# Issuing a request for expert weights only when the last but one of those already issued has landed

## The chip, the cores and the metric

The kernel runs on one core of a Trainium2 chip. The metric is the device time of one execution in microseconds (us), lower is better. Instructions are written by hand for each engine (TensorE = PE, VectorE = DVE, ScalarE = ACT, GpSimd = POOL, SyncE = SP), and the engines wait for each other on semaphores that the code names and counts itself. Transfers from DRAM are requested by SP, almost all of them, in program order, on one hardware queue that 16 DMA engines serve.

## The reference, cut to what matters

Two layers over 256 tokens of 1024 features, in float32. Each layer is a mixing part (gating, attention and retention between two projections) and then a mixture of 16 experts. What bears on the change is the expert part:

```python
for e in range(N_EXPERTS):                      # 16
    he = jax.nn.silu(t @ w_gate[e]) * (t @ w_up[e])
    y = y + combine[:, e:e + 1] * (he @ w_down[e])
```

`w_gate[e]` and `w_up[e]` are 1024 x 512 and `w_down[e]` is 512 x 1024, so each of the three is 2 MB. A token uses two experts, but over 256 tokens all 16 are used, so each layer reads 16 x 3 x 2 MB = 96 MB of expert weights. After the second layer a last RMSNorm is applied.

## The kernel before, in words

The expert part works through **items**. An item is a pair of experts with up to 64 tokens (slots) for each; there are 8 items a layer with these inputs, 16 in all. For an item PE makes the gate product, the up product (both line 1106), turns the hidden tile, and makes the down product (line 1135). It needs three weight tiles of 4 MB: gate, up and down, each requested in two parts of 2 MB. For most items (`load_experts`, lines 417 to 423) the parts are the two experts. For items 1, 2 and 3 and for every fourth item (`load_halves`, lines 403 to 415) they are the two halves of the rows of both experts, and for up and down of every fourth item the second half is requested as two quarters of 1 MB (line 412), the last of which has a semaphore of its own.

There are two buffers for gate (`gate_b`, `gate_a`, by turns) and one each for up and down. So SP requests the gate of an item when PE is done with the gate of two items before (semaphore `gated`), and up and down when PE is done with the part of the item before (`upped`, `downed`). These waits on used buffers are the only ones that the requests have:

```python
for e in experts:
    sp.dma_start(dst[:, e], src[...]).then_inc(loaded[e].sem, 16)
```

SP runs through one program in order: for layer 0 the mixing weights (`load_piece`, lines 385 to 401), then gate, up and down of item 0 and gate of item 1 (lines 442 to 453), a wait for the number of items (line 455), then lines 471 to 478 for gate of items 2 and 3 and up and down of items 1 to 3, then the loop of line 479 for four items a turn (lines 480 to 486; it runs once a layer here). Then it goes on to the mixing weights of layer 1, which reuse the up and down buffers, and at the end to the four stores of the output (line 492). A request that waits holds back all that follow.

Each request adds 16 to its `loaded` semaphore, one for each DMA engine that has landed its share, and PE waits for the full count before the first product that reads the part (lines 1101, 1103, 1139, 1150 and 1153). A wait of SP is followed by `settle`, an increment of a semaphore that nobody reads.

Of the kernel before, what the change touches and what calls it, by code (L numbers as in the profile page):

```python
# [118 lines left out]
def hybrid_trunk(nc, x_in, norm1, w_in, a_ln_g, a_ln_b, a_ws, a_bs, ret_gn, w_out, norm2, router_g, router_gb,  # L119
                 router_e, router_eb, w_gate, w_up, w_down, final_norm, table, out):  # L120
    ctx = ExitStack()
    with ctx:
# [8 lines left out]
        def settle(eng):  # L131

            eng.sem_inc(settled.sem)
# [10 lines left out]
        gate_w = [gate_b.rearrange("p (e c n) -> p e c n", e=2, c=DC), gate_a]  # L144
# [3 lines left out]
        up_w = sb("up_w", [P, 2, DC, HID])  # L148
        up_at = nc.sbuf_base - 4 * 2 * DC * HID
        down_w = sb("down_w", [P, 2, HC, D])  # L150
# [149 lines left out]
        gate_loaded = [[signal(f"gate_loaded{o}{b}", 16) for b in range(2)] for o in range(2)]  # L300
        up_loaded = [signal(f"up_loaded{b}", 16) for b in range(2)]
        down_loaded = [signal(f"down_loaded{b}", 16) for b in range(2)]
        up_last, down_last = signal("up_last", 16), signal("down_last", 16)

        gated, upped, gate_tanh = signal("gated", 2, 8), signal("upped", 2, 8), signal("gate_tanh", 1)
        gate_open = signal("gate_open", 1)
        he_ready, he_turned, heT_ready = signal("he_ready", 1), signal("he_turned", 1), signal("heT_ready", 1)
        downed, y_summed = signal("downed", 2, 8), signal("y_summed", 1)
# [12 lines left out]
        gate_d = w_gate.rearrange("l (q e) (p c) n -> (l q) p e c n", e=2, c=DC)  # L321
# [55 lines left out]
        @block.sync  # L377
        def _(sp):
            sp.dma_start(x[:], x_in.rearrange("b (t p) d -> p (b t) d", p=P)).then_inc(x_loaded.sem, 16)
            sp.wait_ge(range_zeroed.sem, 1)  # L380
            for l in range(DEPTH):

                first = 0 if l == 0 else sp.value_load(items[0:1, 1:2], min_val=0, max_val=4 * PAIRS * DEPTH)

                def load_piece(j, src):
                    if j < 2:

                        sp.wait_ge(upped.sem, upped.at(first, 0))
                    elif j < 4:

                        sp.wait_ge(downed.sem, downed.at(first, 0))
                    else:

                        sp.wait_ge(projected.sem, projected.at(l, j - 3))
                    settle(sp)
                    if j == BQ:
                        for b in range(2):
                            half = slice(None), slice(4 * b, 4 * b + 4), slice(None)
                            sp.dma_start(piece[j][half], src[half]).then_inc(bq_loaded[b].sem, 16)
                        return  # L400
                    sp.dma_start(piece[j], src).then_inc(piece_loaded[j].sem, 16)

                def load_halves(dst, src, loaded, used, g, q, back=0, quarter=None):

                    quarters = dst.shape[2] // 4
                    for b in range(2):
                        sp.wait_ge(used.sem, used.at(g, b + 1 - back * used.turn))
                        settle(sp)
                        if b == 1 and quarter is not None:
                            for k, signalled in ((2, loaded[1]), (3, quarter)):  # L410
                                rows = slice(k * quarters, (k + 1) * quarters)
                                sp.dma_start(dst[:, :, rows], src[bass.ds(q, 1), :, :, rows].rearrange("q p e c n -> (q p) e c n")).then_inc(signalled.sem, 16)
                            continue
                        rows = slice(2 * b * quarters, 2 * (b + 1) * quarters)
                        sp.dma_start(dst[:, :, rows], src[bass.ds(q, 1), :, :, rows].rearrange("q p e c n -> (q p) e c n")).then_inc(loaded[b].sem, 16)

                def load_experts(dst, src, loaded, used, g, q, back=0, experts=(0, 1)):

                    if used is not None:
                        sp.wait_ge(used.sem, used.at(g, 2 - back * used.turn))  # L420
                        settle(sp)
                    for e in experts:
                        sp.dma_start(dst[:, e], src[bass.ds(q, 1), :, e].rearrange("q p c n -> (q p) c n")).then_inc(loaded[e].sem, 16)

                for j in range(6):
                    load_piece(j, w_in_p[bass.ds(l, 1), :, :, PIECE_COL[j]:PIECE_COL[j] + COLS]
                               .rearrange("l p c n -> (l p) c n"))
                    if l == 0 and j == BK:
                        sp.dma_start(const[:, CONST_FIRST:], table[:, CONST_FIRST:]).then_inc(const_loaded.sem, 16)
                for n in range(2):  # L430
                    if n == 1:

                        sp.wait_ge(gelu_done.sem, gelu_done.at(l, 1))
                        sp.wait_ge(proj_copied_a.sem, proj_copied_a.at(l, CQK))
                        for k in range(4):
                            there, here = slice((k ^ 1) * HD // 2, ((k ^ 1) + 1) * HD // 2), slice(k * HD // 2, (k + 1) * HD // 2)
                            sp.dma_start(work1[there], qkc[here].rearrange("p c t -> p (c t)")).then_inc(swapped.sem, 16)
                    load_piece(6 + n, w_out_p[bass.ds(l, 1), :, :, n * COLS:(n + 1) * COLS]
                               .rearrange("l p c n -> (l p) c n"))

                sp.wait_ge(projected.sem, projected.at(l, BV + 1))
                load_experts(up_w, up_d, up_loaded, upped, first, l * PAIRS, 1)
                sp.wait_ge(attended.sem, attended.at(l, 2))
                settle(sp)
                load_experts(gate_w[0], gate_d, gate_loaded[0], None, None, l * PAIRS)

                load_experts(gate_w[1], gate_d, gate_loaded[1], None, None, l * PAIRS + 1, experts=(0,))
                for n in range(2):
                    sp.wait_ge(out_done.sem, out_done.at(l, T + n + 1))
                    settle(sp)  # L450
                    load_experts(down_w, down_d, down_loaded, None, None, l * PAIRS, experts=(n,))
                    if n == 0:
                        load_experts(gate_w[1], gate_d, gate_loaded[1], None, None, l * PAIRS + 1, experts=(1,))

                sp.wait_ge(items_ready.sem, items_ready.at(l, 1))
                settle(sp)
                last = sp.value_load(items[0:1, 1:2], min_val=PAIRS, max_val=4 * PAIRS * DEPTH)

                def pair(g):
                    return sp.snap((g & (PAIRS - 1)) + l * PAIRS)  # L460

                def load_gate(g, o, load=load_halves):
                    load(gate_w[o], gate_d, gate_loaded[o], gated, g, pair(g), 2)

                def load_up(g, load=load_halves, **quarter):
                    load(up_w, up_d, up_loaded, upped, g, pair(g), 1, **quarter)

                def load_down(g, load=load_halves, **quarter):
                    load(down_w, down_d, down_loaded, downed, g, pair(g), 1, **quarter)

                load_gate(first + 2, 0)
                load_up(first + 1)
                load_down(first + 1)
                load_gate(first + 3, 1)
                load_up(first + 2)
                load_down(first + 2)
                load_up(first + 3, quarter=up_last)
                load_down(first + 3, quarter=down_last)
                with sp.Fori(first + 4, last, 4) as g0:
                    for i in range(3):  # L480
                        load_gate(g0 + i, i % 2, load_experts)
                        load_up(g0 + i, load_experts)
                        load_down(g0 + i, load_experts)
                    load_gate(g0 + 3, 1)
                    load_up(g0 + 3, quarter=up_last)
                    load_down(g0 + 3, quarter=down_last)

            out_t = out.rearrange("b (t p) d -> p (b t) d", p=P)
            for n in range(2):
                for t in range(T):  # L490
                    sp.wait_ge(out_ready[t].sem, n + 1)
                    sp.dma_start(out_t[:, t, n * COLS:(n + 1) * COLS], h[:, t, n * COLS:(n + 1) * COLS]).then_inc(out_stored[t].sem, 16)
            for t in range(T):
                sp.wait_ge(out_stored[t].sem, 32)
# [1119 lines left out]
```

## Time and profile before

| what | us |
|---|---|
| median of 3 runs | 693.33 (692.57 to 695.35) |
| the profiled execution, its own time | 693.77 |
| its span | 692.0 |
| PE busy (share of the span) | 658.4 (95%) |
| DMA packets of SP's queue, share of 16 engines' span | 85.5% |

A busy share is a mean over the span; the expert part of layer 0 lies at about 130 to 340 us and that of layer 1 at about 470 to 680 us. A row of the stretches view gives a stretch in us from the span's start, the busy time of each engine in it with the number of instructions, the granted clock of TensorE (1.00 is full), the share of time in which the 16 DMA engines were busy, and the rate in GB/s. A row of the issues view names the tile, the issuing queue, the kind, the count, the size of each and the time from issue to landing.

### The profile page before, as it was taken

Reading aid. Unit: us, or ns where it says so; the run is one execution under the profiler, and the core shown is the slowest. Engines: PE = TensorE matmul, PEld = TensorE weight load, DVE = VectorE, ACT = ScalarE, POOL = GpSimd, SP = SyncE. Lnnn points to the kernel's source line nnn. Section 1 sums busy time; section 2 is a strip of 40 time slices with the busy share of each in tenths; the row PEclk is TensorE's granted clock in tenths of the full one; section 3 lists DMA queues with packets and bytes.
Section 4 is the critical chain, followed back from the end, with each engine's and each line's share of the span. In section 5 each row is a group of like instructions: output and inputs, shape, how many; then the busy total and the mean of one; then the engine's idle time right before and its main releaser. Section 6 shows DMA issues by size and latency. Waiting matters only on the chain.

```text
span 692.0 us, 9069 instructions
## 1 busy us (share of the span) xinstructions
PE 658.4 (95%) x3466; PEld 383.4 (55%) x3466; DVE 303.0 (44%) x634; ACT 195.9 (28%) x344; POOL 17.4 (3%) x29
## 2 busy tenths in 40 slices
PE   6999999999999997999999999999999999989993
PEld 5888878653443542543488878784543453353431
DVE  3769985611232221321475898673221331231234
ACT  4557543421111210211164564342211111111102
POOL 2110000200000000000001000000000000000000
PEclk9999999999999999999999999999999999999997
DMA  9983259999999999999987341997999999999992
GB/s 332 322 313 107 109 209 429 379 415 403 423 416 423 426 426 430 426 423 419 398 311 240 130 152 32 410 430 322 422 420 421 416 428 427 429 427 425 422 411 83
DMA packets 40906, 241.94 MB, mean 350 GB/s; under 512 B 2688, under 2 KB 2880, under 8 KB 24864
## 3 DMA queue, kind: packets, MB, share of 16 engines
q1 hardware_dynamic: 39680, 239.19, 85.5%
q0 software_dynamic: 1040, 2.04, 1.2%
q8 instruction: 28, 0.46, 0.3%
q10 hardware_dynamic: 144, 0.13, 0.1%
q14 instruction: 14, 0.11, 0.0%
HBM read 239.26 MB, written 1.05 MB: 347 GB/s over the span
## 4 chain that ended last, share of the span: by engine, by line
PE 65%; DMA 22%; DVE 8%; ACT 2%; issue 2%; SPq 0%; DVEq 0%; ACTq 0%
PE psum L1106 24%; DMA up_w<-in_w_up 17%; PE psum L779 16%; PE psum L1135 9%; DMA down_w<-in_w_down 3%; PE psum L1044 3%; PE psum L1083 2%; DVE piece_lo L1220 2%; DMA up_w<-in_w_in 2%; PE psum L1008 1%; PE psum L804 1%; PE psum L759 1%; PE psum L949 1%; DMA x<-in_x 1%; PE psum L868 1%
## 5 line engine op out<-in xcount | busy, mean ns | idle before, releaser
L1106 PE MATMUL psum<-up_w,xT 128*64 128x512 f32 x512 | 114.8, 601 | 8.2 <-DMA up_w<-in_w_up 8.2
L1135 PE MATMUL psum<-down_w,scores 128*64 128x512 f32 x512 | 113.3, 594 | 0.8 <-DMA down_w<-in_w_down 0.8
L779 PE MATMUL psum<-piece_hi,hT_part 128*128 128x512 f32 x320 | 100.3, 394 | 0.0
L1106 PEld LDWEIGHTS psum<-up_w,xT 128*64 128x64 f32 x512 | 39.5, 138 | 80.4 <-issue 76.7
L1135 PEld LDWEIGHTS psum<-down_w,scores 128*64 128x64 f32 x512 | 37.5, 137 | 63.8 <-issue 62.5
L1557 DVE TENSOR_TENSOR y_lo<-psum,y_hi 128x512 fp32r<-128x512 f32 x32 | 22.1, 691 | 102.6 <-ACT y_hi L715 102.6
L779 PEld LDWEIGHTS psum<-piece_hi,hT_part 128*128 128x128 f32 x320 | 58.9, 188 | 12.8 <-issue 1.3
L779 PE MATMUL psum<-piece_lo,hT_part 128*128 128x512 f32 x160 | 62.4, 390 | 0.0
L1106 PE MATMUL psum<-gate_a,xT 128*64 128x512 f32 x256 | 56.4, 593 | 1.1 <-DMA gate_a<-in_w_gate 1.1
L1106 PE MATMUL psum<-gate_b,xT 128*64 128x512 f32 x256 | 56.4, 593 | 0.0
L1536 DVE SCALAR_TENSOR_TENSOR work<-work,psum 128x512 f32<-128x512 f32 x16 | 11.0, 687 | 100.8 <-ACT work L704 100.8
L1539 DVE SCALAR_TENSOR_TENSOR work<-work,slot_scales,psum 128x512 f32<-128x512 f32 x16 | 12.0, 748 | 97.7 <-PE psum L1106 97.7
L715 ACT ACTIVATE y_hi<-psum 128x512 fp32r<-128x512 f32 x32 | 19.1, 597 | 97.1 <-PE psum L1135 97.1
L708 ACT ACTIVATE scores<-psum 128x512 f32<-128x512 f32 x16 | 9.6, 597 | 121.1 <-PE psum L1120 121.1
L1531 DVE TENSOR_TENSOR x<-psum,x 128x512 f32<-128x512 f32 x64 | 40.9, 683 | 3.2 <-PE psum L1083 3.2
L1220 DVE TENSOR_TENSOR piece_lo<-down_w,piece_hi 128x2048 fp32r<-128x2048 f32 x16 | 36.2, 2285 | 10.0 <-ACT piece_hi L560 10.0
L1106 PEld LDWEIGHTS psum<-gate_a,xT 128*64 128x64 f32 x256 | 19.7, 137 | 36.7 <-issue 36.7
L1106 PEld LDWEIGHTS psum<-gate_b,xT 128*64 128x64 f32 x256 | 18.9, 137 | 34.8 <-issue 33.0
L704 ACT ACTIVATE work<-psum,slot_scales 128x512 f32<-128x512 f32 x16 | 11.0, 687 | 89.5 <-PE psum L1106 89.3
L779 PEld LDWEIGHTS psum<-piece_lo,hT_part 128*128 128x128 f32 x160 | 30.0, 188 | 6.5
L560 ACT ACTIVATE piece_hi<-down_w 128x2048 fp32r<-128x2048 f32 x16 | 29.9, 1909 | 4.9 <-DMA down_w<-in_w_in 4.9
L1220 DVE TENSOR_TENSOR piece_lo<-up_w,piece_hi 128x2048 fp32r<-128x2048 f32 x12 | 27.1, 2286 | 2.8 <-ACT piece_hi L560 2.7
(250 smaller groups left out, 860.9 us busy)
## 6 DMA issues: line engine op xcount, KB each, us to landing
up_w<-in_w_up SPq DMA_DIRECT2D x28, 2048.0 KB, 15.4
down_w<-in_w_down SPq DMA_DIRECT2D x28, 2048.0 KB, 14.1
gate_b<-in_w_gate SPq DMA_DIRECT2D x16, 2048.0 KB, 15.9
gate_a<-in_w_gate SPq DMA_DIRECT2D x16, 2048.0 KB, 19.0
up_w<-in_w_in SPq DMA_DIRECT2D x6, 2048.0 KB, 12.7
down_w<-in_w_in SPq DMA_DIRECT2D x4, 2048.0 KB, 20.2
down_w<-in_w_out SPq DMA_DIRECT2D x4, 2048.0 KB, 7.8
up_w<-in_w_up SPq DMA_DIRECT2D x8, 1024.0 KB, 16.0
```

The source lines that it names most:

```text
L560: act.activation(piece_hi[HI_BUFFER[j]][:, 4 * b:4 * b + 4, :], piece[j][:, 4 * b:4 * b + 4, :], ACT.Copy).then_inc(piece_hi_ready.sem, 1)
L704: act.activation(sig, psum[:, 0, :], ACT.Tanh, scale=slot_scales[:, i % 2, 0:1]).then_inc(gate_tanh.sem, 1)
L715: act.activation(y_hi[:, n * COLS:(n + 1) * COLS], psum[:, 2 + n, :], ACT.Copy).then_inc(y_hi_ready.sem, 1)
L779: ins = pe.matmul(o, tokens, w[b][:, c, :], start=(c == 0 and n == 0), stop=(c == DC - 1 and n == len(parts) - 1))
L1044: ins = pe.matmul(gather_out(q, b, c), part[:, t, c, :], pick[:, t, experts].rearrange("p e s -> p (e s)"), start=(t == 0 and part is x_hi ...
L1083: ins = pe.matmul(psum[:, added_bank(i, n, t), :], pickT[:, i % 2, t, :], part[:, n * COLS:(n + 1) * COLS], start=(part is y_hi), stop=(pa ...
L1106: ins = pe.matmul(psum[e * SLOTS:(e + 1) * SLOTS, bank, :], xT[:, c, k:k + SLOTS], w[:, e, c, :], start=(c == 0), stop=(c == DC - 1))
L1135: ins = pe.matmul(psum[e * SLOTS:(e + 1) * SLOTS, 2 + n, :], heT[:, c, e * SLOTS:(e + 1) * SLOTS], down_w[:, e, c, n * COLS:(n + 1) * COLS ...
L1220: V.tensor_tensor(piece_lo[j][part], piece[j][part], piece_hi[HI_BUFFER[j]][part].bitcast(F32), ALU.subtract).then_inc(piece_split.sem, 1)
L1531: V.tensor_tensor(xs, psum[:, added_bank(i, n, t), :], xs, ALU.add).then_inc(x_added.sem, 1)
L1539: V.scalar_tensor_tensor(he, sig, slot_scales[:, i % 2, 1:2], psum[:, 1, :], ALU.mult, ALU.mult).then_inc(he_ready.sem, 1)
L1557: V.tensor_tensor(y_lo[:, ys], psum[:, 2 + n, :], y_hi[:, ys].bitcast(F32), ALU.subtract).then_inc(y_lo_ready.sem, 1)
```

## The change

From `load_up` of item 2 on, every part waits, after its buffer is free, for the landing of an earlier part: part k waits for part k of the tile requested just before. As a tile has two parts, that is the last but one of the parts issued. Gate waits for down of the item before, up for gate, down for up. Where a second half is issued as two quarters, the wait stands before the first of them, and the landing of its fourth quarter is not among the landings waited for.

```diff
+                def landed(before, k):
+
+                    if before is not None:
+                        signals, g, each, ahead = before
+                        sp.wait_ge(signals[k].sem, g * each + (ahead + 16))
+                        settle(sp)
+
-                def load_halves(dst, src, loaded, used, g, q, back=0, quarter=None):
+                def load_halves(dst, src, loaded, used, g, q, back=0, before=None, quarter=None):
...
                         sp.wait_ge(used.sem, used.at(g, b + 1 - back * used.turn))
                         settle(sp)
+                        landed(before, b)
...
-                def load_experts(dst, src, loaded, used, g, q, back=0, experts=(0, 1)):
+                def load_experts(dst, src, loaded, used, g, q, back=0, before=None, experts=(0, 1)):
...
                     for e in experts:
+                        landed(before, e)
                         sp.dma_start(dst[:, e], src[bass.ds(q, 1), :, e].rearrange("q p c n -> (q p) c n")).then_inc(loaded[e].sem, 16)
...
-                load_up(first + 2)
-                load_down(first + 2)
-                load_up(first + 3, quarter=up_last)
-                load_down(first + 3, quarter=down_last)
+                load_up(first + 2, before=(gate_loaded[1], first, 8, 16))
+                load_down(first + 2, before=(up_loaded, first, 16, 32))
+                load_up(first + 3, before=(down_loaded, first, 16, 32), quarter=up_last)
+                load_down(first + 3, before=(up_loaded, first, 16, 48), quarter=down_last)
                 with sp.Fori(first + 4, last, 4) as g0:
-                    for i in range(3):
-                        load_gate(g0 + i, i % 2, load_experts)
-                        load_up(g0 + i, load_experts)
-                        load_down(g0 + i, load_experts)
-                    load_gate(g0 + 3, 1)
-                    load_up(g0 + 3, quarter=up_last)
-                    load_down(g0 + 3, quarter=down_last)
+                    for i in range(4):
+                        load = load_experts if i < 3 else load_halves
+                        load_gate(g0 + i, i % 2, load, before=(down_loaded, g0, 16, 16 * (i - 1)))
+                        load_up(g0 + i, load, before=(gate_loaded[i % 2], g0, 8, i // 2 * 16), **({} if i < 3 else dict(quarter=up_last)))
+                        load_down(g0 + i, load, before=(up_loaded, g0, 16, 16 * i), **({} if i < 3 else dict(quarter=down_last)))
```

`load_gate`, `load_up` and `load_down` pass `before` on. No other engine's program is changed, nor the order, number, size or place of any transfer.

## Rows read from the trace of the kernel before

**Rows 1.** The page: 40 slices of the span, DMA queues, and two lines of DMA issues.

```profile
DMA  9983259999999999999987341997999999999992
GB/s 332 322 313 107 109 209 429 379 415 403 423 416 423 426 426 430 426 423 419 398 311 240 130 152 32 410 430 322 422 420 421 416 428 427 429 427 425 422 411 83
...
q1 hardware_dynamic: 39680, 239.19, 85.5%
...
up_w<-in_w_up SPq DMA_DIRECT2D x28, 2048.0 KB, 15.4
...
gate_a<-in_w_gate SPq DMA_DIRECT2D x16, 2048.0 KB, 19.0
```

**Rows 2.** Stretches: full queue, and the places where it ran thin.

```profile
core 0: us, PE busy (x) PEld busy (x) DVE busy (x) ACT busy (x) POOL busy (x), PEclk, DMA share, GB/s
139.00:156.00 17.00, 17.00 (x112) 8.90 (x110) 3.37 (x6) 4.01 (x10) 0.00 (x0) 1.00 1.01 424
158.00:160.00 2.00, 2.00 (x12) 0.75 (x10) 0.69 (x1) 0.63 (x2) 0.00 (x0) 1.00 0.79 307
270.00:310.00 40.00, 39.05 (x194) 18.40 (x195) 9.49 (x16) 5.42 (x11) 0.00 (x0) 0.96 1.01 426
474.00:476.00 2.00, 2.00 (x12) 0.65 (x10) 0.48 (x3) 0.00 (x0) 0.00 (x0) 1.00 0.00 0
476.00:677.00 201.00, 195.72 (x1004) 84.05 (x1000) 47.39 (x80) 27.82 (x58) 0.00 (x0) 1.00 1.00 418
674.00:677.00 3.00, 3.00 (x18) 1.09 (x14) 0.01 (x1) 0.00 (x0) 0.00 (x0) 1.00 0.55 220
```

**Rows 3.** Waits of PE for transfers, 475 to 692 us.

```profile
PE psum L1106 <- DMA up_w<-in_w_up: 4.7, 4, 2.7
PE psum L1135 <- DMA down_w<-in_w_down: 0.4, 1, 0.4
PE psum L1106 <- DMA gate_a<-in_w_gate: 0.2, 1, 0.2
```

**Rows 4.** SP's issues in order of time: start, us, what (first of each pair).

```profile
148.08 0.37 SPq L415 DMA_DIRECT2D up_w<-in_w_up  x1
156.59 3.80 SPq L415 DMA_DIRECT2D down_w<-in_w_down  x2
222.43 0.81 SPq L423 DMA_DIRECT2D up_w<-in_w_up  x2
236.46 0.33 SPq L423 DMA_DIRECT2D down_w<-in_w_down  x1
262.19 0.33 SPq L423 DMA_DIRECT2D gate_b<-in_w_gate  x1
307.63 0.37 SPq L412 DMA_DIRECT2D up_w<-in_w_up  x1
332.12 0.38 SPq L399 DMA_DIRECT2D up_w<-in_w_in  x1
475.17 3.72 SPq L415 DMA_DIRECT2D gate_b<-in_w_gate  x2
478.50 0.39 SPq L415 DMA_DIRECT2D gate_b<-in_w_gate  x1
```

**Rows 5.** Issues view: issues of 148.08, 156.59, 222.85, 236.46, 262.19, 307.63, 475.17, 478.50 us.

```profile
up_w<-in_w_up SPq DMA_DIRECT2D x1, 2048.0 KB, 12.5
...
down_w<-in_w_down SPq DMA_DIRECT2D x1, 2048.0 KB, 9.6
...
up_w<-in_w_up SPq DMA_DIRECT2D x1, 2048.0 KB, 17.9
...
down_w<-in_w_down SPq DMA_DIRECT2D x1, 2048.0 KB, 9.2
...
gate_b<-in_w_gate SPq DMA_DIRECT2D x1, 2048.0 KB, 28.2
...
up_w<-in_w_up SPq DMA_DIRECT2D x1, 1024.0 KB, 19.8
...
gate_b<-in_w_gate SPq DMA_DIRECT2D x1, 2048.0 KB, 7.3
...
gate_b<-in_w_gate SPq DMA_DIRECT2D x1, 2048.0 KB, 8.9
```

**Rows 6.** The chain that ended last, 651 us to the end: start, us, what.

```profile
651.18 0.05 issue
651.23 0.03 SPq L415
651.25 0.04 issue
651.29 20.61 DMA down_w<-in_w_down
671.90 0.24 issue
672.14 7.19 PE psum L1135 x32
...
687.36 0.66 DVEq L122
```

More of the change, by code:

```diff
@@ L460, in pair, with load_gate, load_up, load_down @@
                     return sp.snap((g & (PAIRS - 1)) + l * PAIRS)
[L462 to L469, printed above, removed]
+                def load_gate(g, o, load=load_halves, before=None):
+                    load(gate_w[o], gate_d, gate_loaded[o], gated, g, pair(g), 2, before)
+                def load_up(g, load=load_halves, before=None, **quarter):
+                    load(up_w, up_d, up_loaded, upped, g, pair(g), 1, before, **quarter)
+                def load_down(g, load=load_halves, before=None, **quarter):
+                    load(down_w, down_d, down_loaded, downed, g, pair(g), 1, before, **quarter)
                 load_gate(first + 2, 0)
```

## The prediction

> **What bounds the kernel now.** I read the 40 slices first. In the expert part of each layer the DMA row stands at 9 throughout, at some 420 GB/s, and 239 MB of the traffic is on SP's one queue [rows 1]. PE is nearly as busy, so the next question is which of the two sets the end. From 476 to 677 us the 16 DMA engines are busy 1.00 of the time, while PE is busy 195.7 of 201 us [rows 2] and its idle time there is spent on transfers, 5.3 us [rows 3]. PE begins the layer with weights already in place, catches up with the stream and then waits for it. The chain agrees: its last transfer, a part of down issued at 651.29, takes 20.6 us, and PE's last down product runs on it [rows 6]. So the end of a layer is the start of its stream of requests plus bytes over rate. From 475.17 on, 40 parts of 2 MB (84 MB) follow; at 418 GB/s that is 201 us [rows 2]. Only a DMA engine that idles, or runs at another rate, can move the end.
>
> **Is the order or the depth of the queue what makes a part late?** The second part of gate issued at 262.19 takes 28.2 us to land [rows 4, 5]. Is that slow sharing, or a line? Two parts issued into a short queue give the unit: 475.17 + 7.3 = 482.5 and 478.50 + 8.9 = 487.4, so 4.9 us per part [rows 4, 5]. With the queue empty (share 0.00 from 474 to 476, [rows 2]) one part takes 7.3 us: 4.9 of transfer and 2.4 fixed. 28.2 less 2.4 is 25.8, or 5.3 parts: it stands behind somewhat over four others and then takes its own 4.9. So requests are served one after the other; a deep queue is waiting time, not a slower transfer. Shortening it makes issue to landing short (about 2 x 4.9 = 10 us) by issuing later, and leaves the landing where it is.
>
> **The change, part by part.**
>
> *Rate with two in flight.* Nothing is removed or reordered; parts are issued later. From 139 to 156 us the trace has this very state by accident: each part is issued with one or two others pending, and the rate is 424 GB/s at share 1.01. With three to five pending, 270 to 310 us, it is 426 at 1.01 [rows 2]. Cost of two instead of five: nothing within 0.5%; the cover is the other part in flight.
>
> *Is the cover long enough?* After the change a part is issued when the last but one lands, so one part, 4.9 us, is left. Off this goes the reaction: 0.24 us from a landing to the waiting engine's start, and 0.11 us from a release to SP's issue [rows 6], together 0.35 as an upper bound for the new wait with its settle. 4.55 us remain, and the fixed time to bridge is 2.4: margin 2.1 us for each of the 64 new waits (per layer 4 tiles x 2 in the part before the loop and 12 tiles x 2 in it). The other rows: the part issued at 236.46 had only the one issued at 222.85 ahead of it, landing 17.9 later at 240.75, a cover of 4.3 us, and it landed at 245.7, one unit later: no loss [rows 4, 5]. But the part issued at 156.59 had a cover of 4.0 us (148.08 + 12.5 = 160.6) and landed at 166.2, 5.6 us after, 0.7 us more than the unit [rows 4, 5]; the engines were busy only 0.79 of 158 to 160 us [rows 2]. So the price of one new wait is bounded by 0 (236.46) and 0.7 us (156.59). I take 0: the new cover of 4.55 us is nearer to 4.3 than to 4.0, and 478.50, with a cover of 4.0 us like the bad case, lost nothing. In all, eight parts of the trace were issued with a single one ahead and a cover of 3.9 to 4.7 us; three of them stand in the rows, seven of the eight lost nothing.
>
> *The Trainium skill, weighed.* The fixed 2.4 us is from an idle memory. "DMA: Bandwidth & Descriptors", section "Latency and other measured facts", says that an access to HBM takes 0.2 us on average and 2 us at high load, which the queue of this kernel has all the time. By that page an estimate of the fixed part is 2.4 + 1.8 = 4.2 us, and the margin is 0.35 instead of 2.1; the sum stays 0, but hardly. The late start at 156.59 would fit it, the one at 236.46 does not show it.
>
> *Fast DMA engines.* A landing counts when the slowest of 16 has landed. At the end of the stream, 674 to 677 us, the share falls to 0.55 while the last part is still coming [rows 2]: some engines are 2 us or more ahead. After the change these wait for the slowest one at each part. That costs nothing as long as the slowest is never idle, and it gives nothing either: the rate falls with the share (220/0.55 = 400 against 418/1.00, and 307/0.79 = 389), so an engine does not get faster when others idle. What is lost is some of their lead, which takes up a delay of one engine; I take 0.3 us a layer, between 0 and the 0.7 of the one such event priced above.
>
> *SP itself.* 64 waits, 64 settles and some register arithmetic, with 24 register waits per layer in the loop. SP waits anyway for buffers; between two issues of a pair it needs 0.4 us [rows 4] against 4.9 a part. Cost 0. Behind SP's new waits stand, in its own queue: the next parts (above), the mixing weights of layer 1 and the output. The last new wait of layer 0 is for the third quarter of up, issued at 307.63 and landed at 327.4; the mixing weights are issued at 332.12 when PE is done with the buffer [rows 4, 5]: 4.7 us to spare. The output is stored after the last product. POOL's and ACT's queues are not passed.
>
> *Who waits for a later issue?* PE alone, and it waits for landings, which stay.
>
> Sum: 0 + 2 x 0.3 = 0.6 us at most on 693.77 of the profiled execution, which is 0.4 above the median of 693.33. Put on the median: 693.9, and as the 0.6 is an upper value I say 693.6.
>
> **The rivals.**
>
> *Slower: the queue runs dry between parts.* Each new wait moves an issue back, that of 262.19 by some 18 us (290.4 less two units), so each part now depends on one cover. Where the fixed time exceeds 4.55 us, all 16 engines stop. For: the event at 156.59. Against: seven short covers of the trace without loss. It decides from a fixed time of 4.6 us. If one wait in eight lost 0.7 us, as one short cover in eight of the trace does, the sum is 64/8 x 0.7 = 5.6 us, so 699.3; if all did, 45 us, which I hold for excluded by the stretch from 139 to 156 us. Chance 0.15.
>
> *Faster: fewer requests in flight make the stream smoother.* Engines kept within a part of each other would all finish together, and the spread of 2 us that is exposed at each layer's end (share 0.55 for 3 us is 1.35 us of full rate) would go. For: the spread is there. Against: idle engines do not speed up the others [rows 2]. If it did come: 2 x 1.35 = 2.7 us, up to 4 with a better rate: 690.5. Chance 0.12, of which I put 0.08 beyond 0.5%, as its price lies on that bound.
>
> *The wait hardly ever binds.* Where buffers come free later than the landing, the change does nothing. At 236.46 the landing wait would have been met already. But most parts are issued with three or more pending (28.2 us is one), so it binds for most. It gives 693.4, inside my forecast.
>
> **How the numbers follow.** Forecast of no change: 0.73, with a range of its own of 692 to 696 (the runs shown spread over 692.6 to 695.4, plus the 0 to 1.4 us of lost lead). Slower rival 0.15, faster rival 0.12. To hold 8 in 10 the range reaches toward the rivals: 690.5 to 698. A measurement of this kernel can tell about 0.5%, 3.5 us, from no change. Slower by more: 0.15. Faster by more: 0.08. Within: 0.77.
>
> **What the changed profile would show.** Issue to landing of the expert parts at about 10 us instead of 15 to 19 [rows 1], with the landings themselves in place; SP's own waits moving from PE to DMA; the stream of layer 1 at share 1.00 and 418 GB/s; PE's wait for transfers still near 5 us. A DMA share under 0.98 in the expert part, or units over 4.9 us, would prove me wrong downward; PE waiting less, or units under 4.9, upward.

## The result: 4.4 us slower

| | us |
|---|---|
| before, median of 7 runs | 693.15 (691.82 to 695.35) |
| changed, median of 7 runs | 697.53 (697.27 to 699.71) |
| ratio, 95% interval | 1.0071 (1.0062 to 1.0080) |
| profiled execution of the changed kernel | 697.49, span 695.7 |

The time lies in the range of the prediction (690.5 to 698) and on the side of its first rival: the prediction put 0.77 on a change within 0.5%, and the kernel is 0.7% slower.

The page of the changed kernel, its DMA slices, queues, last chain and issues, against [rows 1]:

```profile
DMA  9993269999999999999997441997999999999992
GB/s 336 326 325 108 82 240 432 359 425 418 411 369 408 425 423 418 424 415 410 401 342 214 155 152 32 389 431 323 423 421 420 411 425 428 419 430 424 421 412 84
...
q1 hardware_dynamic: 39680, 239.19, 85.4%
...
PE 47%; DMA 40%; DVE 8%; ACT 2%; issue 2%; SPq 0%; DVEq 0%; ACTq 0%
...
up_w<-in_w_up SPq DMA_DIRECT2D x28, 2048.0 KB, 9.9
...
gate_a<-in_w_gate SPq DMA_DIRECT2D x16, 2048.0 KB, 11.2
```

From issue to landing a part takes 9.9 us instead of 15.4, and the packets are the same, so the change does what it says. DMA stands at 9 as before. But the rate of slices 11 and 12 (about 174 to 209 us) is 411 and 369 GB/s where it was 423 and 416. The stretches view of the changed kernel:

```profile
139.00:156.00 17.00, 17.00 (x110) 8.89 (x108) 3.36 (x6) 4.01 (x10) 0.00 (x0) 1.00 1.01 426
160.00:180.00 20.00, 20.00 (x102) 8.01 (x100) 4.51 (x7) 1.73 (x4) 0.00 (x0) 1.00 1.01 421
185.00:211.00 26.00, 24.51 (x120) 10.25 (x118) 6.82 (x13) 2.93 (x6) 0.00 (x0) 1.00 0.99 378
270.00:310.00 40.00, 37.19 (x194) 16.93 (x191) 8.19 (x14) 5.51 (x11) 0.00 (x0) 1.00 1.00 419
480.00:680.00 200.00, 195.67 (x994) 84.08 (x992) 47.41 (x80) 27.83 (x58) 0.00 (x0) 0.99 1.00 419
678.00:681.00 3.00, 3.00 (x16) 1.17 (x14) 0.00 (x0) 0.00 (x0) 0.00 (x0) 1.00 0.42 169
```

and of the kernel before, for the stretch that was not shown:

```profile
185.00:211.00 26.00, 25.58 (x128) 10.22 (x126) 7.09 (x14) 2.92 (x6) 0.00 (x0) 1.00 1.01 419
```

Up to 180 us, where the first new wait binds (the up of item 2, issued at 175.10 instead of 170.32), the two streams agree. From 185 to 211 us the changed one has 378 GB/s against 419, with the share of busy time almost the same, 0.99 against 1.01. From 270 to 310 it is 419 against 426 [rows 2]. In this profiled execution layer 0 ends its stream 3.0 us later (last landing 343.1 against 340.1 us). From first landing to last, layer 0 takes 242.6 us against 238.8 and layer 1 238.4 against 238.2, so nearly the whole loss of this execution is in layer 0. The chain that ended last now goes through SP, where the new waits are seen:

```profile
646.08 9.54 DMA gate_a<-in_w_gate
655.66 0.05 issue
655.71 0.03 SPq L423
655.74 0.04 issue
655.77 9.79 DMA up_w<-in_w_up
665.60 0.04 issue
665.64 0.03 SPq L423
665.67 0.04 issue
665.71 9.92 DMA down_w<-in_w_down
```

From a landing to the next issue 0.15 us pass (655.62 to 655.77), less than the 0.35 of the prediction. SP is not what costs the time.

**Where a landing is late.** I took the landing of each part less that of the part before it. The median step is 4.9 us (parts by expert), 4.97 (halves) or 2.55 (quarters); a step longer by over 0.12 us is a late landing. From 180 us in layer 0 and from 510 us in layer 1 the kernel before has 3 of them, 1.3 us together; the changed kernel has 13, 6.6 us together. Of these 6.6 us, 6.2 are at parts in whose last 1.5 to 9.5 us an instruction fetch of 8 or 16 KB began. Such windows cover 42% of the stretches, so a coincidence would give 2.8; moved by a common time, the fetches reach 6.2 us in under 1% of the shifts. The other traces agree: with two in flight in the loop only, or with the idle code of experiment 4, 10 and 12 late landings, 5.4 and 5.2 us together; with three and four in flight 4 and 2, 2.1 and 0.5 us together. One pair, the changed kernel first (issues of 166.19 and 175.10, DMA queues of 179 to 181.5 us), then the kernel before (issues of 166.89 and 170.32, same stretch):

```profile
gate_a<-in_w_gate SPq DMA_DIRECT2D x1, 2048.0 KB, 13.8
...
up_w<-in_w_up SPq DMA_DIRECT2D x1, 2048.0 KB, 11.4
...
q8 instruction: 1, 0.02, 2.7%
```

```profile
gate_a<-in_w_gate SPq DMA_DIRECT2D x1, 2048.0 KB, 14.2
...
up_w<-in_w_up SPq DMA_DIRECT2D x1, 2048.0 KB, 15.8
...
q8 instruction: 1, 0.02, 2.7%
```

Changed: 180.0, then 186.5, a step of 6.5 us. Before: 181.1, then 186.1, a step of 5.0. The same fetch of 16 KB is in both (a packet of 1.1 us on one DMA engine); only the changed kernel pays for it. A fetch hits one engine of 16. If that engine is ahead of the slowest, the landing does not move.

Each part has 16 landings, one for each engine, and they show it: one engine fell back by 1.5 us in both kernels, before one that was 2.0 us ahead of the slowest, in the changed kernel the slowest itself. From 160 us up to there no engine of the changed kernel had lacked work, and most had a lead of 1.3 to 2.1 us. So this hit is not the work of the new wait; as far as the trace shows it is chance. What follows it is: the others are now 1.7 to 3.6 us ahead and have only one part to work on, the next being issued at 186.56. From 187 to 189 us, changed, then before:

```profile
187.00:189.00 2.00, 2.00 (x12) 0.65 (x10) 0.00 (x0) 0.00 (x0) 0.00 (x0) 1.00 0.89 328
```

```profile
187.00:189.00 2.00, 2.00 (x12) 0.72 (x10) 0.00 (x0) 0.00 (x0) 0.00 (x0) 1.00 1.02 426
```

Down to 10 of the 16 engines are at work there. Counted over the stretch from 180 us to 5 us before the last landing of layer 0, the kernel before never has fewer than 16 packets in work, nor has three in flight; the changed kernel has fewer for 11.2 us of 158, mostly 14 or 15, and never none.

### The profile page after: what moved, and what is told of

Same layout as the page of the kernel before. It is cut to its first block, busy times and chain, and to the rows that moved or that the text cites. A ratio compares the mean times of both kernels' runs of the same rounds, so it can differ in the third digit from the quotient of the medians.

```text
span 695.7 us, 9150 instructions
## 1 busy us (share of the span) xinstructions
PE 660.0 (95%) x3466; PEld 385.9 (55%) x3466; DVE 303.0 (44%) x634; ACT 196.1 (28%) x344; POOL 17.0 (2%) x29
## 4 chain that ended last, share of the span: by engine, by line
PE 47%; DMA 40%; DVE 8%; ACT 2%; issue 2%; SPq 0%; DVEq 0%; ACTq 0%
PE psum L786 16%; DMA up_w<-in_w_up 13%; DMA down_w<-in_w_down 13%; PE psum L1113 11%; DMA gate_a<-in_w_gate 7%; PE psum L1142 6%; DMA gate_b<-in_w_gate 4%; DVE piece_lo L1227 2%; DMA up_w<-in_w_in 2%; PE psum L1051 2%; PE psum L1015 1%; PE psum L766 1%; PE psum L811 1%; PE psum L956 1%; PE psum L1090 1%
## 5 line engine op out<-in xcount | busy, mean ns | idle before, releaser
L1113 PE MATMUL psum<-gate_a,xT 128*64 128x512 f32 x256 | 58.2, 607 | 2.8 <-DMA gate_a<-in_w_gate 2.8
## 6 DMA issues: line engine op xcount, KB each, us to landing
gate_a<-in_w_gate SPq DMA_DIRECT2D x16, 2048.0 KB, 11.2
```

The lines of the kernel that those rows point to most:

```text
L1113: ins = pe.matmul(psum[e * SLOTS:(e + 1) * SLOTS, bank, :], xT[:, c, k:k + SLOTS], w[:, e, c, :], start=(c == 0), stop=(c == DC - 1))
```

## The experiments

Theory A, the one to test: with two parts in flight the DMA engines that run ahead empty their queue, lose their lead, and so a delay of one engine moves the landing. Theory B: SP's added instructions, or where its code then lies, cost the time.

### 1. The depth: the same waits, met already, or four, three and one in flight

```diff
 waits already met: every `ahead` one turn lower, e.g.
-load_down(g0 + i, load, before=(up_loaded, g0, 16, 16 * i), ...)
+load_down(g0 + i, load, before=(up_loaded, g0, 16, 16 * (i - 1)), ...)
 four in flight: part k waits for part k of the tile two before, e.g.
+load_down(g0 + i, load, before=(gate_loaded[i % 2], g0, 8, i // 2 * 16), ...)
 three in flight: part 0 waits for part 1 of the tile two before, part 1 for part 0 of the tile before
 one in flight: part 0 waits for part 1 of the tile before, part 1 for part 0 of its own tile
+part, (signals, g, each, ahead) = (0, before[0]) if k == 1 else (1, before[1])
+sp.wait_ge(signals[part].sem, g * each + (ahead + 16))
```

> The same 64 waits, settles and register arithmetic as the change, but each waits for the landing of one turn earlier, which the wait for the used buffer already implies, so no request is held back. Theory A (the two-part cover is too short: DMA engines that run ahead idle and lose their lead): no loss, 693.2 us, ratio 1.000 +- 0.002. Theory B (SP's added instructions, or where its code then lies, cost the time): as slow as the change, 697 to 698 us, ratio 1.006 or more.

> Each part waits for the landing of the part four before it instead of two before, with the same number of waits. Cover about 14.6 us instead of 4.8. Theory A: within 0.2% of before, 692.5 to 694.5 us; issue to landing about 19 us. Theory B: 697 to 698 us as the change.

> Each part waits for the part three before it. Cover about 9.7 us. Theory A: most of the loss gone, 693 to 695 us, as the slowest start seen in the trace (about 5 us after the issue) is covered twice. Theory B: 697 to 698 us. A third view, that a fixed number of requests in the queue and not their cover matters, would put it halfway, near 695.5.

> Each part waits for the landing of the part just before it, so the fixed time of a request lies bare at each of 64 waits. By the fixed time with an empty queue (2.3 to 2.4 us) and 0.1 us of reaction: 64 x 2.5 = 160 us less some 8 where the fourth quarters overlap, so 835 to 855 us, if the fixed time is the same as with an empty queue. If it is longer for some DMA engines, as the late starts suggest: above 855.

| kernel | median us | ratio to before, interval |
|---|---|---|
| waits already met | 693.67 | 1.0003 (0.9994 to 1.0012) |
| four in flight | 693.31 | 1.0002 (0.9993 to 1.0011) |
| three in flight | 693.72 | 1.0004 (0.9995 to 1.0014) |
| two in flight (the change) | 697.53 | 1.0071 (1.0062 to 1.0080) |
| one in flight (2 runs) | 865.7 | 1.2484 (1.2450 to 1.2518) |

Theory B falls: the same instructions with nothing to wait for cost nothing that the interval shows (under 0.8 us). The traces tell how many of the 64 waits held SP back until a landing: none when already met, 19 with four in flight, 45 with three, 62 with two. The loss is the shallow queue, and it is gone at three. Three in flight, stretches view:

```profile
185.00:211.00 26.00, 25.91 (x128) 10.31 (x126) 6.82 (x13) 2.92 (x6) 0.00 (x0) 1.00 1.02 419
270.00:310.00 40.00, 39.52 (x204) 18.61 (x200) 10.48 (x17) 5.84 (x13) 0.00 (x0) 0.96 1.01 426
```

These are the rates of the kernel before to the digit. One in flight measures the fixed time by itself, as it lies bare at each wait and the queue is empty there. Its issues of 246 to 340 us (parts by expert, expert loop of layer 0), and the stretch:

```profile
up_w<-in_w_up SPq DMA_DIRECT2D x4, 2048.0 KB, 7.6
down_w<-in_w_down SPq DMA_DIRECT2D x4, 2048.0 KB, 7.6
...
246.00:340.00 94.00, 61.65 (x266) 25.67 (x268) 12.48 (x21) 7.49 (x16) 0.00 (x0) 0.82 0.74 268
```

7.6 less 4.9 is 2.7 us, and the whole loss says about the same: (865.7 - 693.35)/64 = 2.7 us a wait, with 0.15 us of SP and some instruction fetches in it. The result is above the 855 us to which the 2.4 us of the prediction led. That is no effect of load. The 2.4 is from a part in halves (packets of 8 KB), and in halves one in flight takes 7.2 us, no more than the 7.3 of [rows 5]; a part by expert (16 KB) took 7.6 us in the kernel before too, where the queue was empty. Part by expert issued at 93.66 before, then part in halves issued at 187.28 with one in flight:

```profile
up_w<-in_w_up SPq DMA_DIRECT2D x1, 2048.0 KB, 7.6
...
up_w<-in_w_up SPq DMA_DIRECT2D x1, 2048.0 KB, 7.2
```

### 2. Where the waits stand

```diff
 before the loop only: `before=None` for the three calls in the loop
 in the loop only: `before=None` for the four calls ahead of it
```

> The new waits only at the four tiles before the loop (16 of the 64 waits, all on parts in halves, 8 KB packets). By the landings of the profile of the change, layer 0 fell 1.6 us behind in this part and layer 1 did not: expected 694 to 695.5 us. If the loss goes by the number of waits alone: 693.3 + 4.4/4 = 694.4. If it is all here (halves are what starves the queue): 697.

> The new waits only in the loop (48 of 64, mostly on parts by expert, 16 KB packets). By the landings of the change's profile 1.4 us in layer 0 and 0.9 in layer 1: 695 to 696.5 us. By the number of waits 696.6. If halves alone starve the queue: 693.3.

Before the loop only: 693.89 us, ratio 1.0005 (0.9996 to 1.0013). In the loop only: 696.28 us, 1.0037 (1.0024 to 1.0050). So 16 waits cost 0.6 us, inside the noise and just under the range that I expected, and 48 cost 3.0, as expected; halves alone are not the cause. The profile had misled me here, as it had put 1.6 us of layer 0 ahead of the loop: how much a single execution loses, and where, varies. That fits a loss made of events that hit or miss.

### 3. Copies on one DMA engine

```diff
+for i in range(first_item, first_item + PAIRS):
+    for part, used in enumerate((gated, upped)):
+        pool.wait_ge(used.sem, used.at(i, 2))
+        pool.dma_start(hits[2 * i + part:2 * i + part + 1, 0:8191], x_flat[:, 0:8191]).then_inc(hit_done.sem, 16)
```

> The kernel before, and GpSimd issues 32 copies of 32 KB from DRAM to a scratch in DRAM, two in each item, each one row of 8191 numbers, meant to keep one DMA engine busy for 1 to 2 us. The output is the same. Lead theory (with a deep queue an engine that is delayed has a lead to lose, so delays of different engines do not add up): the 32 copies cost about their mean over the 16 engines, 32 x 1.5 / 16 = 3 us, at most 10: 694 to 703 us. Rival theory (every delay of an engine counts in full at any depth): 32 x 1.5 = 48 us, 741. If the copies all fall on the same engine, also some 48 us, and the pair says nothing.

> The changed kernel with the same 32 copies. Lead theory: with two parts in flight the leads are cut short, so the copies cost clearly more than they cost the kernel before: the difference of the two kernels grows from 4.4 us to 10 or more. Rival theory (a landing is late because the slowest engine itself runs dry after an issue, whatever other engines do): the difference stays at 4 to 5 us.

> Three parts in flight, with the 32 copies, which all fell on one DMA engine and left it up to 13 us behind the others. Before with copies 726.5 us, the change with copies 740.0. If the gap of 13.6 us comes from the cover after an issue (other engines start late while one lags, and lose their lead), a cover of 9.7 us closes most of it: 726 to 730 us. If a lagging engine costs time whenever the wait is for the slowest of the 16, at whatever depth: 735 or more.

| with copies | median us | ratio to the plain kernel before |
|---|---|---|
| before | 726.47 | 1.0477 (1.0461 to 1.0493) |
| three in flight | 732.45 | 1.0577 (1.0555 to 1.0600) |
| two in flight | 740.03 | 1.0667 (1.0645 to 1.0689) |

The 16 copies of 1.2 us of a layer all seem to have fallen on the same engine. In the kernel before one landing of the 16 falls back step by step, to 13.5 us behind the first and 11.7 behind the last but one at the end of layer 0, and both layers become 16 to 17 us longer. So that engine pays for nearly all copies at any depth: 33 us. That is what I had said would tell nothing, but it does tell: the gap grew from 4.4 to 13.6 us. From 250 to 300 us, before, three and two in flight:

```profile
250.00:300.00 50.00, 44.41 (x226) 20.59 (x222) 11.19 (x18) 6.47 (x14) 1.51 (x3) 0.97 1.01 428
```

```profile
250.00:300.00 50.00, 44.11 (x224) 20.39 (x220) 11.16 (x18) 6.47 (x14) 1.51 (x3) 0.97 1.00 403
```

```profile
250.00:300.00 50.00, 43.58 (x217) 20.50 (x219) 10.60 (x18) 5.87 (x13) 1.51 (x3) 0.93 0.99 387
```

With one engine behind, a wait for the slowest of 16 lets the others run dry, and the rate falls with the depth, 428, 403, 387 GB/s, at shares of 1.01, 1.00 and 0.99: in this stretch 2 of 1297 packets of 16 KB took over 1.3 times the median of 0.61 us, then 61 of 1219, then 92 of 1171. For three in flight I expected 726 to 730 and got 732.5: a cover of 9.7 us is no full cure once an engine is that far behind.

### 4. Idle code on GpSimd

```diff
 first try: 512 `pool.nop()` in each of items 0 to 6; second try:
+for _ in range(8 * 64):
+    pool.sem_inc(idle.sem)
```

> The kernel before, and GpSimd runs 512 instructions that do nothing in each of items 0 to 6 of both layers, so that about 28 more instruction fetches of 8 or 16 KB fall into the two streams. The output is the same. Lead theory (a fetch delays one DMA engine by about 1 us, each time another one, and a deep queue lets the engines absorb it): 694 to 697 us, 1 to 4 more than before. Rival theory (every fetch counts in full at any depth): 28 us more, 721.

> The changed kernel with the same idle code. Lead theory: the fetches are only partly absorbed, so the gap to the kernel before with the same code grows from 4.4 us to 9 to 20, that is 704 to 716 us. Rival theory (the loss of 4.4 us does not come from delays of single engines): the gap stays at 4 to 5 us. If the extra fetches are absent or always delay the same engine, the pair says little.

> The kernel before, and GpSimd counts up semaphores that nobody reads, 512 times in each of items 0 to 6 of both layers (7168 instructions), to bring real instruction fetches into the two streams; the idle code tried before brought none. The output is the same. Lead theory: with a deep queue the extra fetches (14 to 56, by their size) are absorbed: 693 to 696 us. Rival theory (a delay of an engine counts at any depth): 10 us more or above. If the trace shows no extra fetch, the pair says nothing again.

> The changed kernel with the same code. Lead theory: the gap to the kernel before with this code grows from 4.4 us to 7 or more, as fetches are nearly doubled or more. Rival theory (each new wait costs by itself): the gap stays between 3.5 and 5.5 us.

The nops brought no fetch into the trace (28 fetches of 16 KB as before): 692.69 us before (0.9996, 0.9987 to 1.0006), 697.11 changed (1.0055, 1.0035 to 1.0075). The pair says nothing of fetches; it repeats the gap, 4.4 us. The counting did bring them. The page's instruction queues, kernel before and changed:

```profile
q8 instruction: 28, 0.46, 0.2%
q14 instruction: 70, 0.57, 0.2%
```

```profile
q8 instruction: 28, 0.46, 0.3%
q14 instruction: 71, 0.58, 0.2%
```

But the code took longer than the layers, and GpSimd set the end: 782.03 and 782.17 us (1.1283 and 1.1290), so the totals are no measure of the streams. The landings are. From first to last landing layer 0 takes 249.1 and 249.8 us, layer 1 249.1 and 251.2, where the plain kernel before takes 238.8 and 238.2. Some 20 more fetches of 8 KB a layer (24 against 4 in 120 to 350 us) cost the deep queue 10 to 11 us, about 0.5 us each, where their packets take 0.3; in it one engine falls behind step by step, to 10.7 us at the end of the layer. So they seem not to go from engine to engine, and my expectation of 693 to 696 failed on that. In the changed kernel the spread between first and last engine stays at about 3 us, and the gap between the kernels is 0.7 and 2.1 us a layer, 2.8 in all. I had expected 7 or more by the theory of the fetches and 3.5 to 5.5 by its rival; neither came. An engine that is behind in small steps costs the shallow queue little more than the deep one, where copies of 1.2 us at a time cost it much more.

### 5. Fewer fetches by PE

```diff
+if c % 4 in (1, 2):      # gate and up; for down: if c in (1, 2)
+    continue
```

> The kernel before without half of the expert products: rows chunks 1, 2, 5 and 6 of gate and up and chunks 1 and 2 of down are left out, so the output lacks their part. All transfers stay. PE's program in the experts is some 45% shorter, and so is the number of its instruction fetches there (8 a layer now, 4 or 5 expected). The stream of weights sets the time: 685 to 693 us.

> The changed kernel without the same products. Lead theory (the loss is the instruction fetches that the DMA engines no longer absorb): with about half the fetches the gap to the kernel before with the same cut falls from 4.4 us to 1.5 to 3. Rival theory (each new wait costs a little by itself, whatever is fetched): the gap stays at 4 us or more, as all 64 waits now bind.

The kernels leave out part of the expert products. PE has 2698 instead of 3466 matmuls, and 10 fetches of 16 KB in the two streams instead of 16. Before 691.62 us (0.9982, 0.9971 to 0.9993), changed 694.95 (1.0033, 1.0022 to 1.0045): the gap is 3.3 us. In proportion to the fetches it would be 2.75, in proportion to the waits 4.4. The intervals, some 0.8 us for each kernel, hold both. The total is also not the streams alone. In the profiled executions (690.54 and 692.81 us, 2.3 apart) the changed kernel loses nothing in its streams: from first to last landing 237.7 and 236.2 us against 237.9 and 236.4, with 3 late landings against 2 (1.7 us each), and its engines had work nearly all the time (15 of 16 at the least). The difference stands behind the last landing, where the granted clock of PE was lower; chain and stretch, before, then changed:

```profile
674.15 1.95 PE psum L1140 x8
...
674.00:676.00 2.00, 1.85 (x8) 0.57 (x8) 0.10 (x1) 0.60 (x1) 0.00 (x0) 1.00 0.00 0
```

```profile
674.44 3.60 PE psum L1147 x8
...
674.00:676.00 2.00, 1.56 (x4) 0.59 (x6) 0.00 (x0) 0.00 (x0) 0.00 (x0) 0.60 0.00 0
```

So 1.7 us of the 2.3 are matmuls at a lower clock. How much of the gap of the medians is clock, one profiled execution of each kernel cannot tell. Inconclusive by the time; the streams are on the side of the fetches, as all 64 waits still held SP back there.

## Why the prediction was wrong

*What bounds the kernel, and the order of the queue*: right. The stream of parts sets each layer's end, parts are served in order, and issuing later shortened issue to landing to 9.9 us (forecast: about 10) with the step between landings still 4.9 us.

*SP itself, cost 0*: right, by the waits already met (1.0003).

*Is the cover long enough, price 0*: right for the usual case, wrong in what it measured. All short covers that I had collected are of the last landing, thus of the slowest engine. Its cover is 4.75 us against a fixed time of 2.3 us (halves) or 2.7 (by expert), and it does not run dry. But an engine that is 2 us ahead has, by an estimate from these numbers, a cover of only 2.75 us: it is at the edge at every part. The trace fits: with leads of about 2 us one or two engines lack work for 0.1 to 1 us after several landings. The event at 156.59, with its share of 0.79 [rows 2], was this case, and I weighed it by the landings alone.

*The Trainium skill* ("DMA: Bandwidth & Descriptors", section "Latency and other measured facts"): its access time to HBM at high load, 2 us, had led to an estimate of 4.2 us for the fixed time. The runs show 2.3 and 2.7 us, but all of them with an otherwise empty queue; no run here shows the fixed time of a request under load by itself, so the estimate is neither borne out nor excluded.

*Fast DMA engines, 0.3 us a layer*: **the step that failed.** The mechanism stood there, lead that is lost and no longer takes up a delay of one engine, and its price was bounded by one event of 0.7 us. It measured 2.2 us a layer as a mean (4.4 over two layers), the slow packets of the next paragraph included. In the sum it stood as 0.6 us for both layers, and this is the term that was too small, by a factor of seven. I counted one event where the stretches have 21 instruction fetches of 0.3 to 1.1 us that a deep queue absorbs almost wholly (late landings of 1.3 us in all) and the shallow one no longer does (6.6 us in the profiled execution). That the fetches are the delays is the reading that fits best, not one that is shown. The fetches stood in the trace as a queue of their own, and I did not look at them.

*That an engine loses nothing but idle time*: wrong as well. I read from the shares that the rate falls with the share. From 185 to 211 us it fell by 10% at a share of 0.99. A queue that has run empty starts again with slow packets, which count as busy: with one in flight the first packets of 16 KB after the issue of 254.01 took 0.8 to 1.8 us each, then 0.61. From 185 to 211 us of the changed kernel 71 of 953 packets of 8 KB took over 1.3 times the median of 0.31 us, up to 2.1 us, against 0 of 1071 before. From 180 us to the end of the stream of layer 0 such excess over the median makes 5.3 us as a mean of the 16 engines against 2.1 before, and engines without work make 1.0 us against 0. Together that is about the 4.1 us by which this stretch is longer, and three quarters of it are slow packets. The quotients of the prediction, 400 and 389 against 418, already showed them: I read them as "not faster" and passed over that they are 4 and 7% slower.

*The rivals*: slower by a queue that runs dry had the right sign and 5.6 us against 4.4; its mechanism, all 16 engines stopped at one wait in eight, was not seen: from 180 us to 5 us before the last landing of layer 0 at least 10 were at work at any time. Faster by a smoother stream did not come: the spread at the end of the stream is still there (share 0.42 for 678 to 681 us).

What stays open: whether the fetches are all of the loss (the coincidence in the traces and the streams of experiment 5 speak for most of it, neither proves it, and the added fetches of experiment 4 cost less than the theory asked for); and why a delay of 1.2 us at a time on one engine costs a shallow queue more than several of 0.4. A wait for, say, the first of the 16 engines instead of the last would have tested the lead by itself; it wasn't tried, as the program would have waited on a count that a transfer passes half-way.

## What to carry to other kernels

Where a stream of transfers sets the time, the depth of its queue is not waste: the time from issue to landing is only a place in the line, and the spare requests let 16 engines drift apart so that what hits one of them is not paid by all. By an estimate from these runs, a limit on requests in flight must leave the *fastest* engine its fixed time after an issue, here 2.7 us beyond a spread of 2 to 3 us, thus three parts of 4.9 us and not two (693.7 against 697.5 us); with an engine 10 us behind, as in experiment 3, three were not enough either. To read whether it does, compare GB/s, not the busy share.

## What the runs showed of the hardware

- The fixed time of a 2 MB request into an empty queue is 2.7 us in packets of 16 KB (7.6 us to landing) and 2.3 us in packets of 8 KB (7.2 to 7.3 us), in the kernel before and with one in flight alike.
- The first packets of 16 KB into an empty queue take 0.8 to 1.8 us where 0.61 is the median (one in flight, issue of 254.01), and the busy share does not show it.
- PE's instruction fetches (16 KB, packets of about 1.1 us) set one DMA engine back by 1.5 us (landings of 186.1 before and 186.5 changed). They seem to fall on changing engines, as the deep queue's spread stays at 2 to 3 us; GpSimd's (8 KB) behaved as if always on one (spread of 10.7 us after 24 of them).
- The copies of one row issued by GpSimd behaved as if all 16 of a layer used the same DMA engine (spread of 13.5 and 13.0 us at the ends of the layers).
